# Layer 0 attention: every third unit a context unit, and banded scores over 128 rows with zero-filled keys

## What is computed

```
# layer 0, in even_mixer: 8 MLA heads and 8 banded heads (2 key groups of 64 columns)
k_all = concat([ck_m, lk_m]);  v_all = concat([cv_m, lv_m])
o_mla = full_attention(lq_m, k_all, v_all)                       # x queries, 768 keys
o_swa = window_sink_attention(lq_s, lk_s, lv_s, ck_s, cv_s, sink)  # band of +-128 keys, and ctx
o_mla_c = full_attention(cq_m, ck_m, cv_m)                       # ctx queries, 256 keys
o_swa_c = ctx_sink_attention(cq_s, ck_s, cv_s, sink)             # ctx queries, 256 keys, a sink
# softmax with a sink: m = max(s.max(), sink); e = exp(s - m); e / (e.sum() + exp(sink - m))
h_lat = h_lat + gate * (concat(o_mla, o_swa) @ w_out);  h_ctx the same
```

## Time and profile before

| | us |
|---|---|
| median of 3 runs | 2685.73 (2684.48 to 2693.44) |
| the profiled execution, its own time | 2680.81 |
| its span in the trace | 2679.0 |
| attention, first scores to the start of the next stage | 267.57 to 532.71 |

### The profile page before, as it was taken

The page is one execution under the profiler, slowest core; times in us unless marked ns, Lnnn a source line. Parts: engine busy times, 40 slices in busy tenths (PEclk is TensorE's granted clock), DMA queues, the critical chain, the costliest instruction groups (busy, mean ns, idle before and its releaser), DMA issues. The chain is left out here.

```text
span 2679.0 us, 34002 instructions
## 1 busy us (share of the span) xinstructions
PE 2367.4 (88%) x13438; PEld 1243.9 (46%) x13438; DVE 864.2 (32%) x1691; ACT 653.7 (24%) x1413; POOL 276.2 (10%) x257
## 2 busy tenths in 40 slices
PE   7999999798899999999992789997879989898864
PEld 3554554376544333333330778885744333333321
DVE  2332566635710000000003945555461000000005
ACT  1111444432012121111211344444311211111111
POOL 1000000032011111111110000000211111111100
PEclk9999999798999999999996989999979999999987
DMA  8565200022479999999984711100346999999967
GB/s 323 199 227 189 95 1 1 11 81 87 171 300 350 380 392 388 393 372 376 382 320 166 279 36 36 37 24 1 146 194 261 420 407 416 419 414 404 396 262 298
DMA packets 122204, 646.54 MB, mean 241 GB/s; under 512 B 18648, under 2 KB 29912, under 8 KB 60352
## 3 DMA queue, kind: packets, MB, share of 16 engines
q1 hardware_dynamic: 92512, 556.21, 53.1%
q0 software_dynamic: 29248, 87.12, 8.3%
q10 hardware_dynamic: 288, 1.05, 0.1%
HBM read 604.38 MB, written 57.75 MB: 247 GB/s over the span
## 5 line engine op out<-in xcount | busy, mean ns | idle before, releaser
L1530 PE MATMUL E_psG<-E_gu,E_xT 128*32 128x512 f32 (+2 forms) x2576 | 534.5, 618 | 40.6 <-DMA E_gu<-in_we_up_dram 24.4
L1824 DVE TENSOR_TENSOR E_hh<-E_sil,E_psG 128x256 f32<-128x256 f32 x96 | 40.4, 421 | 1094.1 <-ACT E_sil L1663 1094.1
L1530 PE MATMUL E_psG<-o,E_xT 128*32 128x512 f32 (+2 forms) x912 | 280.4, 626 | 21.6 <-DMA E_gu<-in_we_up_dram 21.6
L1530 PEld LDWEIGHTS E_psG<-E_gu,E_xT 128*32 128x32 f32 (+2 forms) x2576 | 158.8, 123 | 262.9 <-issue 256.4
L1544 PE MATMUL E_psY<-E_dn,E_hT 128*32 128x512 f32 (+1 forms) x1288 | 261.8, 596 | 1.5 <-ACT E_hT L1666 1.5
L1663 ACT ACTIVATE E_sil<-E_psG 128x256 f32<-128x256 f32 x96 | 36.8, 383 | 670.0 <-PE E_psG L1530 670.0
L1405 POOL DMA_INDIRECT y_d<-E_yb,E_sca x94 | 94.1, 1001 | 995.9 <-ACT E_yb L1669 985.8
L1669 ACT ACTIVATE E_yb<-E_psY,E_wgt 128x1024 f32<-128x1024 f32 x96 | 106.9, 1114 | 289.5 <-PE E_psY L1544 289.5
L1530 PE MATMUL E_psG<-raw,E_xT 128*32 128x512 f32 (+2 forms) x464 | 148.3, 594 | 1.2 <-DVE E_xT L1821 1.2
L1530 PE MATMUL E_psG<-fT,E_xT 128*32 128x512 f32 (+2 forms) x496 | 148.4, 594 | 0.5 <-ACT E_xT L1660 0.5
L1544 PE MATMUL E_psY<-o,E_hT 128*32 128x512 f32 (+2 forms) x456 | 134.4, 596 | 0.0
(11 more groups left out here) (387 smaller groups left out, 3688.2 us busy)
## 6 DMA issues: line engine op xcount, KB each, us to landing
E_gu<-in_we_gate_dram SPq DMA_DIRECT2D x78, 1024.0 KB, 11.0
E_gu<-in_we_up_dram SPq DMA_DIRECT2D x78, 1024.0 KB, 14.7
E_dn<-in_we_down_dram SPq DMA_DIRECT2D x78, 1024.0 KB, 15.2
h<-in_w_ada_dram SPq DMA_DIRECT2D x40, 1024.0 KB, 4.6
o<-in_we_gate_dram SPq DMA_DIRECT2D x26, 1024.0 KB, 10.3
o<-in_we_up_dram SPq DMA_DIRECT2D x26, 1024.0 KB, 15.1
o<-in_we_down_dram SPq DMA_DIRECT2D x26, 1024.0 KB, 12.7
I_ring<-y_d SPq DMA_DIRECT2D x24, 1024.0 KB, 7.0
```

The source lines that it names most:

```text
L1530: ins = nc.tensor.matmul(psG[c:c + n, 0].rearrange("p (v f) -> p v f", v=2), xT[:, k, c:c + n], slots[s][0][:, :, k], start=(k == 0), stop ...
```

## The change

**Order of units.** A list `seq` replaces the plain order: two units of x, then one of ctx, 32 times. The x units keep their order (16 such threes with MLA, 16 with banded heads); the ctx units (quads from `FIRST` = 16 on) keep theirs, so MLA ctx units lie between MLA x units and banded between banded. `last`, `done`, `nth` and `end` give each quad its last step, its place in the order of completion and the step of its last values matmul. A quad of x still has its values in quarters over four steps; a quad of ctx has all of them in one step.

**Room.** The turned probabilities of ctx quads lie in `h[:, NL:NT]`, so ctx is no longer loaded into `h` at the attention's start but in `stage_out`, ahead of `D_brt` and `D_wr`; those who add to it wait for a new semaphore.

**Banded scores.** `C_kz` holds for each key group all 128 rows, those of the other group set to zero (POOL fills it once at the stage's start). The banded scores contract over 128 rows.

**Reciprocal.** It is taken of 4 columns, and a copy spreads the result over 256.

```diff
+            seq = []
+            for n in range(N // 3):
+                seq += [divmod(2 * n, 4), divmod(2 * n + 1, 4), divmod(4 * FIRST + n, 4)]
+            last = [seq.index((Q, 3)) for Q in range(NQ)]
+            done = sorted(range(NQ), key=lambda Q: last[Q])
+            nth = [done.index(Q) for Q in range(NQ)]
+            end = [last[Q] + 6 for Q in range(NQ)]
...
-                        sp.dma_start(h[:, NL:NT], a["ctx"][0].rearrange("(t p) d -> p t d", p=P)).then_inc(s_h, 16)
...
+                    @block.gpsimd
+                    def _(pool):
+                        nc.gpsimd.memset(kz[:], 0.0).then_inc(s_z, 1)
+                        pool.wait_ge(s_z, 1)
+                        for g in range(SKV):
+                            own = slice(SD * g, SD * g + SD)
+                            nc.gpsimd.tensor_copy(kz[own, g], ksT[own]).then_inc(s_kz, 1)
...
-                                q, kT = qsT[64 * g:64 * g + 64, j, t * P:(t + 1) * P], ksT[64 * g:64 * g + 64]
+                                q, kT = qsT[:, j, t * P:(t + 1) * P], kz[:, g]
...
-                            if i >= 6:
-                                values((i - 6) // 4, (i - 6) % 4)
+                            for Q in done:
+                                for part in range(4):
+                                    if i == (end[Q] - 3 + part if Q < FIRST else end[Q]):
+                                        values(Q, part)
...
-                            link(V.reciprocal(rsum[:, Q % 2], bcl(sl, MV)), s_rs)
+                            link(V.reciprocal(rcp[:], sl))
+                            link(V.tensor_copy(rsum[:, C % 2], bcl(rcp[:], MV)), s_rs)
...
+                        if nt > NL:
+                            sp.dma_start(h[:, NL:NT], a["ctx"][0].rearrange("(t p) d -> p t d", p=P)).then_inc(s_hc, 16)
                         sp.dma_start(brt[:], a["b_router"][l:l + 1, :].to_broadcast([P, NE])).then_inc(s_br, 16)
```

More of the change, by code:

```diff
@@ L744, in stage_attend0 @@
                 sdif = sb(ctx, "C_sdif", [P, 2, 4])
+                rcp = sb(ctx, "C_rcp", [P, 4])
+                kz = sb(ctx, "C_kz", [P, SKV, NT * P])
                 rsum = sb(ctx, "C_rsum", [P, 2, 4, MV])
@@ L753, in stage_attend0, with turned, read_of @@
                 s_rs, s_b, s_bs = sem("C_rs"), sem("C_b"), sem("C_bs")
-                windows = [Q for Q in range(NQ) if quads[Q][0] == 1]
+                s_z, s_kz = sem("C_z"), sem("C_kz")
+                windows = [Q for Q in done if quads[Q][0] == 1]
+                first_window = min(i for i in range(N) if quads[seq[i][0]][0] == 1)
+                def turned(Q):
+                    return pTs[0 if Q < FIRST else 1][:, Q % 2]
+                def read_of(Q):
+                    return nth[Q - 2] + 1 if Q >= 2 and Q != FIRST and Q != FIRST + 1 else 0
                 def place(n, b):
@@ L815, in values @@
                                     v = vM[:, ks[n], hd * MV:(hd + 1) * MV] if kind == 0 else vS[:, ks[n], hd // 4 * SD:hd // 4 * SD + SD]
[L816 removed]
+                                    ins = nc.tensor.matmul(psO[64 * s:64 * s + 64, C % 2, 0].rearrange("p x n -> p (x n)"), v, turned(Q)[:, s, n],
                                                            start=(n == 0), stop=(n == len(ks) - 1))
@@ L879, in _ @@
                                 maximum(i)
[L880 to L885 removed]
+                            for w, Q in enumerate(windows):
+                                if i == last[Q] + 1:
+                                    hd = 2 * quads[Q][2]
+                                    if w >= 2:
+                                        dve.wait_ge(s_se, w - 1)
+                                    link(V.tensor_tensor(sdif[:, w % 2], sink[:, hd:hd + 4], nmax[:, Q], ALU.add), s_sd)
                             if 2 <= i < N + 2:
                                 evac(i - 2)
[L888 to L891 removed]
+                            for Q in done:
+                                if i == last[Q] + 3:
+                                    sums(Q)
+                                if i == end[Q] + 2:
+                                    divide(Q)
                     @block.scalar
```

98 lines of the change are left out of this document (53 added, 45 removed).

## The result

| | before | changed |
|---|---|---|
| median of 4 runs each, us | 2685.11 (2683.26 to 2693.44) | 2663.24 (2657.82 to 2667.37) |
| the profiled execution, us | 2680.81 | 2665.35 |
| its span, us | 2679.0 | 2663.6 |
| attention, first scores to the next stage, us | 265.1 | 242.5 |

The ratio is 0.9909, with a 95% interval of 0.9887 to 0.9931: faster by 0.9%. Forecast were 2662, a gain of 23.7 (21.9 measured), and an attention of about 240 us.

What follows compares the result with a forecast made beforehand. PE's own work bounds the x stretches, a copy chain the ctx stretches. Gains of 22 (to the last scores) and 2.2 (end), less 0.5 (later load), make 23.7: 2685.7 - 23.7 = 2662 us, range 2655 to 2668.

Steps and rivals of the forecast that it cites:

- 24.2 less 0.5: Whole program: 22 us up to the last scores and 2.2 at the attention's end, less 0.5 for the later bias load.
- The attention's end: After the last scores: the same work or one ctx quad's values more, at full clock, 8.5 us against 10.7.
- The banded rounds: Banded half in six-step rounds: 14.2 us with 5 tiles, 12.4 with 4, four of each, 106 us.
- The chain L: End of a unit's score columns to earliest next transposes, DVE and ACT free: 2.70 or 2.49 us for MLA x.
- the waits worked out from it: PE idle before transposes in an MLA round: 0.72, 0.35 and 0.26 us in steps 1, 2 and 5, 1.3 in all.
- So there are two things to win: Ctx stretches of the attention: idle PE time in 73 us of ctx work, and the half clock in the last 34.
- the MLA rounds: MLA half in six-step rounds: 15.6 us each, times 8, 125 us.
- The ctx chain: Ctx stretches: the next turn needs the copied-out result, and ACT's half of that copy stands behind the next unit's exp.
- The short reciprocal frees DVE: Division over 4 columns: DVE is late nowhere in the new order, so the gain is nothing.
- 12 to 13 us forecast: Banded x scores over 128 rows: weight loads no longer exposed, 0.42 us per x unit; the prediction itself put 12 us on it.
- The paragraph on the Trainium skill: Banded scores: the page implies 128 rows gain nothing, costing 12 us; the trace's 0.62 against 0.44 us pair was held against it.
- The rival in which it spreads: New rounds fall to 1.2 GHz: gain gone from 53 us at half clock, 2698 us at 80; chance 0.04.

Runs made afterwards that it cites:

- the swap: ACT's copy of unit i-2 put ahead of its exp of unit i, against the changed kernel: 2646.73 us, ratio 0.9858; a second time 2638.7 us.

## Why the prediction was right, and where its reasons were not

**The total and the attention.** 2662 was forecast and 2663.24 measured. That is nearer than the parts were: of the forecast gain of 23.7, 24.2 less 0.5, the attention gave 22.6 in the first trace and 24.9 in the second, and the medians 21.9. In the two profiled executions, 15.5 us apart, the attention gained 22.6, and 4.6 went back in the stage behind the first `D_y` (three long tiles against none), 0.4 ahead of it and about 2 in the rest. But what lies behind the attention took 2152.8 and 2149.2 us in two traces of the changed kernel, 2157.8 and 2150.4 in two of the one with the swap, and 2137.3 with the short reciprocal alone, against 2146.3 before: it moves by several us from one execution to the next, and the medians' 21.9 are close to the attention's gain. So most of the loss behind belongs to the execution; that none belongs to the kernel is not shown.

The attention's end took 10.25 where 8.5 were forecast, with 3.4 us of half clock that the forecast left out; in the second trace, without it, 8.6. The banded rounds took 2.5 more than forecast.

**Interleaving: rounds right, credit wrong.** The chain L and the waits worked out from it came in within 0.1 to 0.2 us for each step, since they were built from rows of the same instructions. But "So there are two things to win: idle PE time in 73 us of ctx work, and the half clock in its last 34" gave the new order some 11 of the 24 us, and the old order with all the other edits is as fast (239.0 against 242.5 and 240.2). The prediction's own figures could have told half of this. It put 125 us on the MLA rounds, and the MLA stretches of before add up to 124.5: no gain there. What it compared the banded rounds with were ctx units at half clock and behind long divisions, and both have a cheaper cure.

**The ctx chain: one link missed.** "`turn(i-1)` needs `C_psP` copied out, and the ACT half of that copy stands behind the exp of the next unit" was right, and the swap shows it: the attention is 22 to 23 us shorter, 21 of them in the rounds. That exp was in turn held up by DVE's 1.74 us reciprocal, once per quad. "The short reciprocal frees DVE, which is late nowhere in the new order: nothing" was 6.5 us of attention off in the new order, in the banded rounds, and the prediction looked only there; on the kernel before the same edit is worth 16.9. This step failed, though the total came in: the edit was costed in the new order alone, so the order got the credit of it.

**128 rows.** 12 to 13 us forecast, 12.6 measured in the banded part of the new order; 0.34 for the scores and 0.06 for the transposes of a unit of x (0.42 forecast). The reading as weight loads that are not hidden at a change of rows is shown by the loads themselves and by the MLA scores over 64 rows. The paragraph on the Trainium skill set 0.62 against 0.44 as a disagreement; the 0.62 belongs to the changes around the matmul, and a 64-row matmul among its like takes what one over 96 rows takes.

**The half clock.** It all but left the banded ctx units with either of the two small edits in the old order (0.94 with 128 rows, 1.00 with the short reciprocal, 1.00 with both). Why the banded ctx units at 64 rows with long reciprocals lost it and the MLA ctx units with the same waits did not, no run settles. The rival in which it spreads did not come: no banded round of the changed kernel runs below 1.00.

**D_brt.** 17.1 for 17.2 forecast, waiting for `D_brt` as forecast, 0.6 later than PE alone would have let it start (0.5 forecast). With `D_brt` first the wait ends on PE again. That the start hardly moved against the run with the swap alone (17.3 and 17.4) is no sign against it: PE's last product came late in both, at 17.1 and 17.2.

## What to carry to other kernels

When a change has several parts, cost each on the kernel before as well as on the changed one: a sum can be right while the name on it is wrong, and here all the other edits in the old order reached the full gain, and each of the two smallest alone gave two thirds of the attention's gain or more. Before units are interleaved to fill an engine's idle time, read what stands ahead of the late instruction in the queue of the engine that is waited for; moving one copy ahead of one exp removed the waits that the interleaving only moved. A division spread over many columns belongs on the few columns that differ, and matmuls that alternate should use the same rows of PE.

## What was not expected of the hardware

- DVE's fp32 reciprocal takes 1.74 to 1.75 us for 256 columns and 0.17 to 0.18 for 4; the copy that spreads the four takes 0.29.
- Each change between matmuls over 64 and over 128 rows costs 0.1 to 0.25 us of PE, 0.13 to 0.17 in the mean; between 96 and 128 rows nothing was seen.
- In the projection stage the clock falls to 0.50 for 3.41 us at the start of some tiles, 0 to 4 of the five behind the first, differently in two executions of one kernel; each such tile is 1.55 us longer.
